# A wait between the first and the second row gather of a mixture-of-experts stage

## The reference, cut to what matters

```
g_idx = argmax(t @ w_rg + b_rg)                  # one of 4 expert groups
top_w, top_i = top_k(softmax(e_logits[g_idx]), 2)  # two of its 8 experts
for e in range(32):
    hid = silu(t @ w_gate[e]) * (t @ w_up[e])    # 1024 -> 256
    y = y + combine[:, e:e+1] * (hid @ w_down[e])  # 256 -> 1024
```

## Time and profile before

| | |
|---|---|
| median of 3 runs | 715.65 us (714.64 to 716.02) |
| the profiled execution's own time | 714.52 us |
| its span, first to last instruction | 712.8 us |
| mean granted clock of TensorE | 0.998 |
| busy: PE, DVE, ACT, POOL | 694.9, 555.1, 451.9, 154.3 us |
| gathers, scatters | 32 and 32, one indirect DMA each |
| HBM over the span | 162.89 MB read, 34.39 MB written |

### The profile page before, as it was taken

The page is one execution under the profiler, slowest core; times in us unless marked ns, Lnnn a source line. Parts: engine busy times, 40 slices in busy tenths (PEclk is TensorE's granted clock), DMA queues, the critical chain, the costliest instruction groups (busy, mean ns, idle before and its releaser), DMA issues.

```text
span 712.8 us, 11964 instructions
## 1 busy us (share of the span) xinstructions
PE 694.9 (97%) x3846; PEld 543.7 (76%) x3846; DVE 555.1 (78%) x890; ACT 451.9 (63%) x714; POOL 154.3 (22%) x157
## 2 busy tenths in 40 slices
PE   8999999999999999999988999999999999999995
PEld 6687877887778777767777888888888888888842
DVE  4785776866868875363886999999999999999857
ACT  6746345364465642223236888898889888898744
POOL 0110010010110221000014233333333333331124
PEclk9999999999999999999999999999999999999999
DMA  8985730330311636646438999999999999998758
GB/s 329 285 220 215 170 90 21 68 88 0 88 59 67 239 118 243 232 148 189 113 137 352 415 413 413 406 381 395 407 389 377 384 398 393 369 412 324 275 189 353
DMA packets 80970, 181.10 MB, mean 254 GB/s; under 512 B 41760, under 2 KB 46032, under 8 KB 72744
## 3 DMA queue, kind: packets, MB, share of 16 engines
q1 hardware_dynamic: 71432, 163.12, 63.0%
q0 software_dynamic: 9216, 16.93, 6.3%
q10 hardware_dynamic: 288, 0.62, 0.2%
HBM read 162.89 MB, written 34.39 MB: 277 GB/s over the span
## 4 chain that ended last, share of the span: by engine, by line
PE 87%; DVE 5%; DMA 3%; issue 2%; ACT 2%; POOL 1%; SPq 0%; DVEq 0%; ACTq 0%; POOLq 0%
PE psZ L1439 24%; PE psZ L944 19%; PE psS L1466 12%; PE psZ L1140 10%; PE psT L836 6%; PE psOG L836 2%; PE psOG L1020 2%; PE psS L988 2%; DMA wo_in<-w_out 1%; PE psOG L879 1%; DMA wi_first<-w_in 1%; PE psOG L1271 1%; PE psOG L1029 1%; DVE x1a L2739 1%; PE psT L1229 1%
## 5 line engine op out<-in xcount | busy, mean ns | idle before, releaser
L2435 DVE TENSOR_TENSOR wg_lo<-wg,wg_hi 128x1024 fp32r<-128x1024 f32 x128 | 150.6, 1216 | 2.1 <-ACT wg_hi L1577 2.0
L1577 ACT ACTIVATE wg_hi<-wg 128x1024 fp32r<-128x1024 f32 x128 | 128.9, 1063 | 3.2 <-DVE small L2597 1.6
L1439 PE MATMUL psZ<-wg_hi,xg_hi 128*128 128x512 f32 x252 | 101.4, 402 | 0.0
L1439 PE MATMUL psZ<-wg_hi,xg_lo 128*128 128x512 f32 x252 | 99.0, 393 | 0.0
L1439 PE MATMUL psZ<-wg_lo,xg_hi 128*128 128x512 f32 x252 | 98.9, 393 | 0.0
L2821 POOL DMA_INDIRECT y_d<-y_t,idx_dst x32 | 48.9, 1528 | 188.6 <-ACT y_t L1577 188.6
L2624 DVE TENSOR_TENSOR wd_lo<-wd,wd_hi 128x2048 fp32r<-128x2048 f32 x31 | 71.1, 2292 | 21.1 <-ACT wd_hi L1577 21.1
L944 PE MATMUL psZ<-wi_hi,xT_hi 128*128 128x512 f32 (+1 forms) x224 | 84.1, 376 | 0.0
L944 PE MATMUL psZ<-wi_lo,xT_hi 128*128 128x512 f32 (+1 forms) x224 | 81.9, 366 | 0.0
L944 PE MATMUL psZ<-wi_hi,xT_lo 128*128 128x512 f32 (+1 forms) x224 | 81.9, 365 | 0.0
L2817 POOL DMA_INDIRECT xg<-h_d,idx_src x32 | 58.4, 1826 | 22.7 <-issue 14.2
(11 more groups left out here) (370 smaller groups left out, 1361.8 us busy)
## 6 DMA issues: line engine op xcount, KB each, us to landing
wg<-w_gate SPq DMA_DIRECT2D x32, 1024.0 KB, 10.6
wg<-w_up SPq DMA_DIRECT2D x32, 1024.0 KB, 16.8
wd<-w_down SPq DMA_DIRECT2D x32, 1024.0 KB, 11.6
y_d<-wo_stage SPq DMA_DIRECT2D x1, 4608.0 KB, 16.7
x_t<-x_rows SPq DMA_DIRECT2D x8, 512.0 KB, 4.0
mix_d<-mix_t SPq DMA_DIRECT2D x8, 512.0 KB, 2.9
m_t<-mix_d SPq DMA_DIRECT2D x8, 512.0 KB, 3.9
x1a<-x_rows SPq DMA_DIRECT2D x8, 512.0 KB, 4.8
```

What stands on the lines that cost most here:

```text
L1439: last = nc.tensor.matmul(psZ[z][:], a[:, c, :], w, start=(n == 0), stop=(n == 3 * DC - 1))
L1577: return nc.scalar.activation(out, in_, ACT.Copy)
L2435: tt(wg_lo[k][:, :, c, :], wg[k][:, :, c, :], wg_hi[p][:].bitcast(F32), ALU.subtract).then_inc(s_wgl, 1)
```

## The change

POOL issues the gather of expert 0, waits until its rows have landed, and then issues those of experts 1 to 4. Nothing else is changed.

```diff
             pool.wait_ge(s_idx, 1)
-            for e in range(5):
+            gather4(0)
+            pool.wait_ge(s_ga[0], 16)
+            for e in range(1, 5):
                 gather4(e)
             pool.wait_ge(s_idx, 3)
             for e in range(NE):
                 stage4(e)
```

## The result

| | before | with the change |
|---|---|---|
| median | 715.03 us (21 runs) | 716.76 us (21 runs) |
| lowest to highest | 712.86 to 717.49 | 715.47 to 718.59 |
| ratio | | 1.0026, 95% interval 1.0019 to 1.0034 |
| profiled execution: its time, span | 714.52, 712.8 | 717.59, 715.8 |
| mean granted clock of TensorE | 0.998 | 0.995 |

The kernel became slower by 0.26% of 715.03, 1.9 us. That is a little more than the 0.2% taken as the limit of what counts as a change, and the interval reaches to just under it. The prediction's range held it (716.76 in 715.1 to 717.9). As a time, 716.76 lies in the likeliest case, A (716.0 to 717.1); but those times stood on 715.65 for the kernel before, and that came out at 715.03. By the difference, 1.9 us, and by PE's wait, 2.0 us, it was rival C that came about.

A forecast was written before the change was run, and what follows sets the result against it. The prediction took PE (TensorE) to bound the kernel, 87% of the span. Gather 0's gain of 0 plus a 1.0 us stall on expert 1's rows, added to 715.65, gave 716.65, taken as 716.6 us; range 715.1 to 717.9.

The forecast's parts named there:

- A: Forecast case at expert 1's rows: PE stalls partly, 0.3 to 1.43 us, time 716.0 to 717.1 us; chance 0.47.
- rival C: Gather 1 pays a whole q1 turn or a 1.99 us issue: stall 1.5 to 2.5 us, 717.15 to 718.15; chance 0.30.
- What bounds the stage: Expert stage: PE, 87% of the span, has no later idle time, so an early delay reaches the end whole.
- Gather 0 gains nothing: Gather 0 on q0: its packets already have the queue alone, so gain 0, at most 0.4 us.
- POOL's new doorbell: POOL's issue of gather 1: starts at 378.58, takes 0.99 us, doorbell at 379.57, 1.7 us later than before.
- The place behind SP's loads: Gather 1 on q0: its doorbell now falls behind SP's six loads on q1, where before it slipped in ahead.
- From doorbell to PE: Gather 1's transfer: rows in PE's hands at 385.6 to 386.0, stall 0.6 to 1.0 us, taken as 1.0.
- two discounts: Gather 1's transfer: q0's turn comes at 382.2 to 382.6 whoever rang first, and 0.14 MB needs 0.5 us less.
- the heavy end: Gather 1 as slow as gather 2 before: 6.94 us from doorbell to PE, rows at 386.51, stall 1.50 us.
- Loads at no cost: SP's weight loads on q1: lose 0.5 us or so to gather 1, cost 0, covered by two experts of prefetch.
- Gathers 2 to 4 at no cost: Later gathers on POOL: gather 2 in hand at 389.6, PE wants it at 392.02 + 1.0; cost 0.

The follow-up runs named there:

- e3: The change plus ten spare matmuls on PE before its wait for expert 1's rows; 1.0014 of the kernel before.
- e10: Second measurement of e2's kernel (POOL's wait between gathers 1 and 2); 1.0005 of the kernel before.
- e2: The change with POOL's wait for gather 0 moved to between gathers 1 and 2; 0.9990 of the kernel before.
- e5: Kernel before, no POOL wait, SP's loads of experts 2 and 3 issued ahead of gather 0; 1.0092 of the kernel before.
- e9: The change, with SP's six loads also held until PE has transposed expert 0's rows; 1.0013 of the kernel before.
- e4: The change, but POOL waits for the transposes of expert 0's rows instead of their landing; 1.0040 of the kernel before.
- e8: The change, but POOL waits for the first piece of expert 0's gate and up instead of gather 0's landing; 1.0043 of the kernel before.
- e1: The change, with SP's loads of experts 2 and 3 also held until gather 1 has landed; 1.0042 of the kernel before.
- e12: Kernel before with six more spare matmuls in PE's wait for gather 0; 1.0010 of the kernel before, 714.74 against 713.84 us.
- e6: The change, SP's loads meant to follow a semaphore POOL raises behind gather 1's issue, but they were not held; 1.0026 of the kernel before.
- e7: The changed kernel measured a second time, nothing else altered; 1.0025 of the kernel before.
- e11: Kernel before, without POOL's wait, SP's six loads held until expert 0's rows are transposed; 1.0005 of it, 714.57 against 714.33 us.

## Why the prediction was right or wrong, point by point

- **What bounds the stage: right.** The delay of expert 1's rows, 2.2 us, is still 2.1 at the end of the stage in e3. The pause ahead of the first down matmuls moves along, as the prediction said, when the rows are late; it shrinks only where the clock slows PE alone, by 0.44 us in the change.
- **Gather 0 gains nothing: right as far as can be told.** Its link is 4.03 us before and 3.65 after. But e10 and e2 issue gather 1 at once, as before: e10 has 377.84 - 374.04 = 3.80 to PE's start, and in e2 SP's first load goes 379.33 - 375.70 = 3.63 behind the start of gather 0's issue. So the 0.38 is mostly the spread between executions.
- **POOL's new doorbell: right,** 1.27 us behind the landing for 1.20; the issue took 1.00 us and not 1.99.
- **The place behind SP's loads: right,** and the heart of the matter. e5 shows it with the loads alone, e9 shows POOL's wait without it and no stall, and e2 and e10 have the old time with gather 1 ahead of the loads.
- **From doorbell to PE: this is the step that failed.** I took 6.0 to 6.4 us, by two discounts on the heavy end of 6.94: that q0's turn comes at a moment set by q1, and that a smaller gather is through sooner. It was 7.53. First, the turn did not stay at a fixed moment: the first packets came 3.5 us behind gather 1's own doorbell, where 2.6 to 3.0 were forecast, and moved with the doorbell in e4 and e8. The second and larger error is in how I read the packets. I took gather 2's end from the moment at which 144 packets of q0 had begun. After the change 145 had begun by 386.3, yet PE's wait ended at 387.61, 1.3 us later. In the quiet hole of gather 0 such a count ended 0.4 us before the landing. Under load the count of packets did not date the landing, and the forecast had taken 0.37 us for that last part. Only the discount for fewer bytes did no harm: the count itself took 2.7 us where 3.05 were forecast. Even the heavy end, 6.94, was too low. The stall was 2.04 us where I forecast 1.0.
- **The clock: left out.** The forecast has no term for it and names no reason. It fell in both profiles of the change and cost 1.3 us up to expert 2's transposes, some 0.8 by the end of the stage; in e3, with PE busy throughout, it did not fall there.
- **Loads at no cost: right in the result, wrong in the reason.** The cover was about half a microsecond by the estimate from e1, not two experts.
- **Gathers 2 to 4 at no cost: right.** No wait of PE on a later gather appears.
- **Forecast against rival C.** C had the right mechanism for the stall and a chance of 0.30; it has no clock either. Its condition, rows in hand after 385.01 + 1.43 = 386.44, was met: 387.61, or 387.2 when the later start of 0.44 us is taken off.
- **The number: near by luck.** The forecast of 716.6 is 0.2 us from the measured 716.76. But the effect was 1.9 us and not 1.0, and the kernel before came out 0.6 us lower than the 715.65 that the forecast stood on; the two errors nearly cancel.

**Open.** In its two profiles the change lengthens the stage by 2.9 us, while 21 timed runs say +1.9. The spread between executions, 712.9 to 717.5 for the kernel before, is wider than the effect. PE's wait for `yy`, none to 1.1 us in these profiles, is one part of it. The clock's falls outside the stall are not borne out as another: of the runs of the kernel before with a clock on record (beside e1 to e12), the 23 with a mean clock of 0.995 or less average 714.6 us and the 57 with 0.997 or more 714.4. What makes up the rest was not found.

The Trainium skill, page "DMA: Bandwidth & Descriptors", section "Queues, rings and completion order", has the DMA engines take the queues in turn, a packet of about 9 to 17 descriptors at a time. The 3.0 to 3.5 us without a packet of q0 behind a doorbell under load agree with a turn that has to be waited for; the packets of a turn were not counted. The same page of the Trainium skill, in the section "Anatomy of one DMA", fits a transfer as 2.0 us plus its bytes at 436 GB/s, by which 0.14 MB would take an estimated 2.3 us. That fits the gather 1 that met an empty q1 (2.3 us in e1) and is short by 4 to 5.5 us for the gathers that did not.

## What to carry to other kernels

A wait put between two transfers that never overlapped is not free: ask what else is released by the same event, here six loads on another queue, and who rings first. Price a late transfer by one of before that met the same traffic, from doorbell to the instruction that used it, and take off nothing that no row shows. Then ask what TensorE's clock did in rows behind idle stretches of that length, and price both.

## What the runs showed of the hardware

- A gather took 2.3 to 2.8 us from its doorbell to its user on quiet DMA engines (2.34 in e1, 2.78 for gather 0 before; 3.2 in e9, where earlier loads still moved beside it), and 6.3 us (e8) to 7.9 us (e5) with SP's loads in front, for the same 144 packets. Some 3.2 to 3.5 us of the latter are time without a single packet of its queue.
- A semaphore that POOL raised behind an indirect DMA in program order released SP at once, before that DMA's issue began (e6, one profile: 377.14 and 377.29).
- TensorE's clock fell to 0.50 for some 3 to 4 us behind every wait for expert 1's rows, 2.0 to 3.5 us long (the change, e7, e6, e4, e8). Behind the wait for gather 0 it stayed at 1.00 in eight profiles (1.57 to 1.97 us) and fell in three (1.89 us in e11, 2.30 in e9, 6.42 in e5), so the length of the wait alone doesn't tell: 1.97 us left it at 1.00 and 1.89 did not. It was also 0.50 from 374 to 378 in e3, with no wait of PE for a gather.
